# Re-ordering the start of a one-core decoder layer: warm-up operand, the add of the mean squares, five positions in four instruction streams

## The reference

```python
h = rmsnorm(x, norm_pre_g)                       # 512 x 1024
u = h @ w_in                                     # 1024 x 4096: q, k, v, gate of two head groups
a = diff_attention(...) * silu(gate_a)           # 4 heads, two softmax maps each, map0 - lam * map1
b = moba_attention(...) * silu(gate_b)           # 8 heads of 64
y = concat(a, b) @ w_out                         # 1024 x 1024
out = x + rmsnorm(y, norm_post_g)
```

## Time and profile before

| | us |
|---|---|
| median of three runs | 254.41 |
| the profiled execution | 254.41 |
| its span, first to last instruction | 252.5 |
| PE busy in the span | 245.4 (97%) |
| DVE busy | 176.8 (70%) |
| ACT busy | 142.8 (57%) |
| POOL busy | 32.2 (13%) |

### The profile page before, as it was taken

The page is one execution under the profiler, slowest core; times in us unless marked ns, Lnnn a source line. Parts: engine busy times, 40 slices in busy tenths (PEclk is TensorE's granted clock), DMA queues, the critical chain, the costliest instruction groups (busy, mean ns, idle before and its releaser), DMA issues.

```text
span 252.5 us, 4454 instructions
## 1 busy us (share of the span) xinstructions
PE 245.4 (97%) x1569; PEld 123.1 (49%) x1569; DVE 176.8 (70%) x393; ACT 142.8 (57%) x336; POOL 32.2 (13%) x74
## 2 busy tenths in 40 slices
PE   7999999999999999999999999999999999999991
PEld 7444444445454554544455444454444454555570
DVE  2898586487468688868877767977787896835313
ACT  4677566165356667574677595667565665611110
POOL 2129300000000320041032033000000000111101
PEclk9999999999999999999999999999999999999998
DMA  7968989605555544544935654679849769982422
GB/s 241 401 203 189 310 269 378 207 6 135 106 163 159 180 114 128 148 155 115 209 96 134 139 159 120 129 186 170 169 130 220 192 158 167 203 202 43 125 86 83
DMA packets 59674, 42.47 MB, mean 168 GB/s; under 512 B 45808, under 2 KB 46072, under 8 KB 59652
## 3 DMA queue, kind: packets, MB, share of 16 engines
q1 hardware_dynamic: 59636, 42.18, 63.9%
q10 hardware_dynamic: 16, 0.00, 0.0%
HBM read 29.04 MB, written 2.13 MB: 123 GB/s over the span
## 4 chain that ended last, share of the span: by engine, by line
PE 93%; DMA 3%; SPq 1%; DVE 0%; DVEq 0%; issue 0%; POOLq 0%; ACT 0%; POOL 0%; ACTq 0%
PE unit_ps L574 72%; PE score_ps L630 6%; PE o_ps L651 5%; PE unit_ps L604 4%; DMA stage<-in_w_in_dram 3%; PE unit_ps L611 2%; PE unit_ps L585 1%; PE score_ps L703 1%; PE unit_ps L703 1%; SPq L364 0%; PE score_ps L532 0%; SPq L395 0%; DVE area L1052 0%; DVEq L180 0%; POOLq L180 0%
## 5 line engine op out<-in xcount | busy, mean ns | idle before, releaser
L574 PE MATMUL unit_ps<-area,w_hi 128*128 128x512 f16 x256 | 76.2, 379 | 0.0
L782 ACT ACTIVATE arena<-arena,negmax 128x512 f32<-128x512 f32 (+3 forms) x64 | 35.4, 554 | 49.6 <-DVE negmax L979 49.4
L574 PE MATMUL unit_ps<-w_hi,area 128*128 128x512 f16 x192 | 60.3, 379 | 0.0
L574 PE MATMUL unit_ps<-area,w_lo 128*128 128x512 f16 x128 | 48.5, 379 | 0.0
L574 PEld LDWEIGHTS unit_ps<-area,w_hi 128*128 128x128 f16 x256 | 24.1, 98 | 27.2 <-issue 1.1
L574 PE MATMUL unit_ps<-w_lo,area 128*128 128x512 f16 x96 | 36.4, 379 | 0.0
L979 DVE CUSTOM_DVE_ANT_0 arena<-score_ps,strips 128x512 f32<-128x512 f32 (+3 forms) x64 | 28.6, 483 | 9.3 <-PE score_ps L630 9.3
L876 DVE SCALAR_TENSOR_TENSOR w_lo<-stage,g_cols,w_hi 128x512 f16<-128x512 f32 x32 | 24.1, 754 | 10.4 <-ACT w_hi L740 10.3
L574 PEld LDWEIGHTS unit_ps<-w_hi,area 128*128 128x128 f16 x192 | 18.8, 98 | 21.9 <-DVE w_lo L882 0.7
L739 ACT ACTIVATE w_hi<-stage,g_cols 128x512 f16<-128x512 f32 x32 | 22.7, 710 | 6.6 <-DMA stage<-in_w_in_dram 6.4
L878 DVE SCALAR_TENSOR_TENSOR w_lo<-stage,g_cols,w_hi 128x512 f16<-128x512 f32 x32 | 24.8, 776 | 0.0
(11 more groups left out here) (106 smaller groups left out, 356.4 us busy)
## 6 DMA issues: line engine op xcount, KB each, us to landing
stage<-in_w_in_dram SPq DMA_DIRECT2D x32, 512.0 KB, 4.1
stage<-in_w_out_dram SPq DMA_DIRECT2D x8, 512.0 KB, 4.3
arena<-in_x_dram SPq DMA_DIRECT2D x4, 512.0 KB, 8.7
strips<-bias_rows SPq DMA_DIRECT2D x4, 512.0 KB, 4.4
stage<-in_x_dram SPq DMA_DIRECT2D x4, 512.0 KB, 4.4
out_dram<-area SPq DMA_DIRECT2D x3, 512.0 KB, 2.8
strips<-bias_rows SPq DMA_DIRECT2D x1, 1024.0 KB, 7.0
pt<-arena SPq DMA_TRANSPOSE x32, 3.1
```

What stands on the lines that cost most here:

```text
L574: last = nc.tensor.matmul(bank, a, b, start=(k == 0 and n == 0), stop=(k == KT - 1 and n == 2))
L782: nc.scalar.activation(probs[:, i % 2, m, 0:n], probs[:, i % 2, m, 0:n], ACT.Exp, bias=negmax[:, i, m:m + 1], scale=-1.0, accum_out=sums[: ...
```

## The change

It does six things. (1) The warm-up multiplies the identity matrix instead of the tile of ones, seven times instead of eight, and so waits for POOL instead of DVE; DVE's memset is gone. (2) The add of the two halves of the mean square moves from DVE to POOL, ahead of POOL's power, for all four tiles. (3) On ACT unit(0) moves ahead of xn_hi(2), and square(3) behind it. (4) On SP quarter 6 is issued behind both transposes of tile 3, not between them. (5) The four strips go in slots 2, 3, 5, 12 instead of 3, 4, 10, 13. (6) `norm_post_g` is loaded in slot 7 instead of 6.

```diff
--- before.py
+++ after.py
@@ -95,10 +95,10 @@
     quarters = iter((u, q) for u in range(FIRST_UNITS, UNITS) for q in range(4))
     FILL = [tuple([next(quarters) for _ in range(n)] for n in share) for share in shares]
     FILL_END = [[u for part in FILL[j] for u, q in part if q == 3] for j in range(SLOTS)]
-    WARM_UP = 8
+    WARM_UP = 7
     STORE_SLOT = {32: 0, 33: 1}
-    STRIPS_SLOT = {3: 0, 4: 1, 10: 2, 13: 3}
-    GPOST_SLOT = 6
+    STRIPS_SLOT = {2: 0, 3: 1, 5: 2, 12: 3}
+    GPOST_SLOT = 7
     LAST_UNIT = UNITS - 1
     FILL_LAST = [uq for uq in quarters if uq[0] < LAST_UNIT]
     FILL_LAST.sort(key=lambda uq: (uq[0] == LAST_UNIT - 1) * (1 + uq[1] // 2))
@@ -253,7 +253,6 @@
         score_ps = ctx.enter_context(nc.psum_tensor("score_ps", [P, 4, 512], fp32))
         o_ps = ctx.enter_context(nc.psum_tensor("o_ps", [P, 2, 512], fp32))
 
-        warm = gates[:, 1, 2, 0:P]
         x_first = gates[:, 1, 0:2, :].rearrange("p t (k s) -> p (t k) s", s=P)
 
         def x_columns(t):
@@ -283,7 +282,6 @@
         split_lo = sem("split_lo")
 
         consts_ready = sem("consts_ready")
-        warm_ready = sem("warm_ready")
         ident_zero = sem("ident_zero")
         x_squared = sem("x_squared")
         x_half_squared = sem("x_half_squared")
@@ -408,9 +406,9 @@
             load_quarter(5)
             for h in range(2):
                 turn_x(2, h)
-            turn_x(3, 0)
             load_quarter(6)
-            turn_x(3, 1)
+            for h in range(2):
+                turn_x(3, h)
             load_quarter(7)
             load_quarter(8)
             sp.dma_start(lam_in[:, :, :], diff_lambda[0].partition_broadcast(P)).then_inc(lam_loaded, 16)
@@ -466,6 +464,10 @@
             pool.wait_ge(consts_ready, 2)
 
             for t in range(TILES):
+                pool.wait_ge(x_squared, t + 1)
+                pool.wait_ge(x_half_squared, t + 1)
+                nc.gpsimd.tensor_tensor(x_ms[:, t:t + 1], x_sq[:, t:t + 1], x_half_sq[:, t:t + 1], ALU.add)\
+                    .then_inc(x_mean, 1)
                 pool.wait_ge(x_mean, t + 1)
                 nc.gpsimd.tensor_tensor(x_rstd[:, t:t + 1], x_ms[:, t:t + 1], minus_half[:, 0:1],
                                         ALU.pow).then_inc(x_rstd_ready, 1)
@@ -536,7 +538,7 @@
             def warm_up(n):
 
                 for _ in range(n):
-                    nc.tensor.matmul(unit_ps[:, 1, 0:P], warm, warm, start=True, stop=True)
+                    nc.tensor.matmul(unit_ps[:, 1, 0:P], ident[:, :], ident[:, :], start=True, stop=True)
 
             def unit_quarter(u, q):
 
@@ -652,9 +654,8 @@
                                                     start=(k == 0 and n == 0), stop=(k == t and n == 2))
                 last.then_inc(values_done, 1)
 
-            pe.wait_ge(warm_ready, 1)
+            pe.wait_ge(consts_ready, 2)
             warm_up(WARM_UP)
-            pe.wait_ge(consts_ready, 2)
             pe.wait_ge(gpre_loaded, 16)
             nc.tensor.transpose(unit_ps[:, 0, 0:KT], g_rows[:, :], ident[0:KT, 0:KT]).then_inc(g_turned, 1)
             pe.wait_ge(x_loaded[0], 16)
@@ -823,9 +824,9 @@
             split(3)
             x_square(2)
             x_hi(1)
+            unit(0)
+            xn_hi(2)
             x_square(3)
-            xn_hi(2)
-            unit(0)
             xn_hi(3)
             for u in range(1, FIRST_UNITS):
                 for n in SPLIT_AT_UNIT[u]:
@@ -930,13 +931,6 @@
                                                scalar=NORM_EPS, op0=ALU.mult, op1=ALU.add,
                                                accum_out=x_half_sq[:, t:t + 1]).then_inc(x_half_squared, 1)
 
-            def x_mean_square(t):
-
-                dve.wait_ge(x_squared, t + 1)
-                dve.wait_ge(x_half_squared, t + 1)
-                nc.vector.tensor_tensor(x_ms[:, t:t + 1], x_sq[:, t:t + 1], x_half_sq[:, t:t + 1],
-                                        ALU.add).then_inc(x_mean, 1)
-
             def x_norm(t):
 
                 dve.wait_ge(x_rstd_ready, t + 1)
@@ -1054,9 +1048,7 @@
                                                    ALU.add).then_inc(y_ready, 1)
 
 
-            nc.vector.memset(warm, 1.0).then_inc(warm_ready, 1)
             x_half_square(0)
-            x_mean_square(0)
             dve.wait_ge(g_turned, 1)
             nc.vector.tensor_scalar(g_cols[:, :], unit_ps[:, 0, 0:KT], W_SCALE, 1.0, ALU.mult,
                                     ALU.mult).then_inc(g_scaled, 1)
@@ -1066,16 +1058,13 @@
             x_norm(0)
             split(0)
             x_half_square(1)
-            x_mean_square(1)
             split(1)
             x_norm(1)
             split(2)
             x_half_square(2)
-            x_mean_square(2)
             split(3)
             x_lo(1)
             x_half_square(3)
-            x_mean_square(3)
             xn_lo(2)
             unit(0)
             xn_lo(3)
```

## The result

The changed kernel takes 255.58 us (six runs, 255.0 to 256.3) against 254.29 before (six runs, 254.08 to 254.54): a ratio of 1.0055, 95% interval 1.0035 to 1.0077. It is 1.3 us slower, above the predicted 254.83 and above the range's end of 255.4.

The account below looks back on a forecast made before the run. TensorE was taken as the bound, waiting for nothing after 11.02 us, so later delays are paid in full. 254.41 plus 0.42 at unit 2, all else 0, gave 254.83; range 254.3 to 255.4 (8 in 10).

Parts of the forecast that it names:

- the sign: Whole run: slower given 0.39, the same 0.54, faster 0.07; what can't be told from no change is 0.5 us.
- the step that was to bring the 0.42: Tile 2: POOL's held add and power delay xn_hi(2), so unit 2 begins at 21.08 instead of 20.66; bounds 0.06 to 0.8.
- Strips and norm_post_g ... 0: Moved loads on the queue: needed much later, cost 0; bound one load's transfer ahead of one transpose, below 1.4 us.
- The misread step: quarter 6: Load behind tile 3's transposes: issued 23.75, landed 27.25 to 27.95, in time for unit 4 until 28.0, cost 0.
- rival A: Quarter 6 lands behind 28.0 and unit 4 stalls: slower, 255.2 at a landing of 28.4; chance 0.18.
- The add on POOL: Tiles 1 to 3: DVE holds POOL's add to about 0.7 us; x_norm(1) 0.38 late, xn_hi(2) at 16.72, unit 2 0.42 late.
- Rival C: POOL not held for the add, or ACT's new order makes up for it: not slower, 254.4; chance 0.20.
- The warm-up: Start of TensorE: 14 passes from about 1.52 us, transposes of tile 0 0 to 0.1 us later, cost 0.
- the cover: TensorE's wait before 11.02 us for the weights' third quarter: 0.3 us that hides a later start.
- Rival B: Clock rises late, at about 7.8 us, so tile 0's transposes and unit 0's first passes run at half: 255.05; chance 0.10.

Follow-up runs that it names:

- b_load6_behind: Kernel before with quarter 6 issued behind both transposes of tile 3, alone: 254.65 us, ratio 1.0003, beside 254.49.
- b_load6_with_pool_act: Kernel before with the add on POOL, ACT's new order and quarter 6 ahead of both transposes of tile 3: 254.72 us, ratio 1.0009.
- b_warm: Kernel before with the new warm-up alone (seven matmuls on the identity): 254.32 us, ratio 0.9998, beside 254.36.
- b_load6_first: Kernel before with quarter 6 issued ahead of both transposes of tile 3, alone: 254.58 us, ratio 0.9998.
- b_strip_slot12: Kernel before with the fourth strip in slot 12 instead of 13, alone: 254.93 us, ratio 1.0015, beside 254.36.
- b_act_order: Kernel before with ACT's new order alone (unit(0), xn_hi(2), square(3)): 254.52 us, ratio 1.0003, beside 254.50.

## Why the prediction was wrong

It forecast 0.42 us more, gave slower 0.39 against 0.54 for the same, and had the wrong place, the wrong size and one edit misread. That the sign came out right is in part luck: the step that was to bring the 0.42 brought 0.34 alone, not clear of zero, and the largest part of the loss came from a step that was put at nothing. Step by step:

*The step that failed: "Strips and norm_post_g ... 0".* The prediction reasoned that transfers needed much later, in a queue whose work never made TensorE wait, can go anywhere. That looks at the moved transfer and not at what stands behind it. The fourth strip was moved from behind the transpose of step 12 to 1.6 us ahead of it; the transpose came 2.2 us later and had 1.4 of slack. The prediction named the right mechanism as its bound, one load's transfer ahead of one transpose, but put it below 1.4 us where it measured 2.2, wrote "all hidden unless the slack there is smaller", and did not read the slack. The kernel before's trace had it, the landing at 125.0 and the values at 126.39; but slack of 1.4 against a bound below 1.4 would still have said nothing, so it is the price that was too small, and the missing reading only hid how close the two were. This edit alone is 0.57 us (1.0001 to 1.0030), and 0.67 in the changed kernel (255.43 against 254.76). The other three strips did nothing that any run shows: in the trace after they stand 4.2, 3.5 and 2.6 us ahead of the next transpose, and the values of steps 0 to 11 are all 0.79 late, no more than unit 4.

*The misread step: quarter 6.* The description of the change in this document, item 4, and the prediction have it issued behind both transposes of tile 3. The diff has it ahead of both. The price given, for a load that is late, was therefore for another edit; b_load6_behind made that one, and there the figures held roughly: issued 24.3 (forecast 23.75), landed 28.1 (27.25 to 27.95), TensorE at unit 4 waiting 0.2 us, 254.65. That wait is rival A, of a load that is late, at its smallest; the changed kernel has none at unit 4. What the real edit does is the same as with the strip: it puts a load 0.6 us ahead of a transpose that TensorE needs some 5 us later. At the median it is worth 0.39 us in the changed kernel (255.15 against 254.76, not clear of the spread), nothing in the kernel before (254.58 twice), nothing in the company of the POOL and ACT parts (ratios 1.0009 against 1.0008), and nothing with the strip in slot 11 (254.84 against 254.87 with the quarter behind). In single profiles it is 0.5 (the trace after) and 1 us (b_load6_with_pool_act). So this part of the loss is seen in traces and not shown by the times.

*The add on POOL: mechanism right, size too large.* The adds of tiles 1 to 3 took 0.56 to 0.71 us where 0.7 was forecast, and the power of tile 1 ended at 11.84 (forecast 12.1, with the tile 0.16 us earlier). x_norm(1) came 2.47 us behind the tile's arrival on DVE instead of 2.21: 0.26 late, not 0.38. xn_hi(2) began at 16.33 (16.72), unit 2 at 20.91, 0.25 late (0.42). At the end of the run 0.34 us for both parts, within its uncertainty of zero. What the Trainium skill says in "SBUF — State Buffer", section "SBUF: two separate sides", of an exclusive lock held for a whole instruction agrees with the records: each add of tiles 1 to 3 ends about when DVE's two-operand instruction does (10.81 and 10.77 us for tile 1), and the powers of tiles 1 and 2 behind it wait out the next one. Rival C, a POOL that is not held, is out by the same records.

*The warm-up: cost right, cover right.* The transposes of tile 0 came 0.22 us late rather than 0 to 0.1, and the cover took it; b_warm is at 0.9998.

*Rival B, the clock.* It happens, but no run shows that the change brings it. All 14 warm-up records of the changed kernel are at the slow duration, and so are all 16 in most profiles of the old warm-up:

```profile
L541 PE MATMUL unit_ps<-ident x14: 421/421/581, 1.5 to 4.5; 128*128 128x128 f32 x14
```

```profile
L539 PE MATMUL unit_ps<-gates x16: 421/421/580, 1.0 to 4.4; 128*128 128x128 f32 x16
```

The first is the changed kernel, the second b_load6_first, which has the warm-up of before. The profile read for the prediction, with its shortest record of 294 ns, was one of two early ones among ten profiles of the old warm-up (the other is b_strip_slot12's, shortest 274 ns). In the other eight, and in all eight of the new one, the rise came behind the warm-up, in the transposes or in unit 0, and unit 0 began between 6.57 and 6.99 instead of 6.05 and 6.29. Eight of eight against eight of ten is no proof that the new one is later, and b_warm costs nothing. In eleven of these sixteen the spacing of tile 0's transposes falls from 0.21 to 0.11 us within the eight, so the clock did rise in a stretch of transposes, which the prediction had left open. TensorE's clock level in the warm-up is 1.2 GHz by the spacing of 0.21 us between passes of 128 columns, and 2.4 where it is 0.11.

*What is accounted for.* Of the 1.1 to 1.3 us, the strip makes 0.57 to 0.67. Quarter 6 makes between nothing and 0.4. With both as before 0.18 is left, which may be nothing, and with both out of the way in another place 0.38, which is not; how that part divides no run here shows.

## What to carry to other kernels

Where the bound engine never waits, price each moved transfer by the transfers that stand behind it in the same queue: their landing, their reader's start, and the slack between the two, each from the trace of before. Take the price of a load ahead wider than the nearest row gives it (below 1.4 us there, 2.2 here). A slot or two in a list of issues can be worth more than an instruction moved between engines. And read a diff of order twice, once for what leaves a place and once for what is now in front of what.

## What was not expected of the hardware

A transpose issued within 2 us behind a load lands behind that load, however early it is issued: 0.76 to 1.05 us behind it in the eleven pairs that the moved strip and quarter 6 make (125.2 and 125.9 in b_strip_slot12; 26.2 and 27.1 in b_load6_with_pool_act), and up to 2.9 in the other pairs of these profiles (26.5 and 29.4 in b_act_order). The load itself is late too: the fourth strip took 4.2 us in slot 13 of the kernel before, 4.6 to 5.0 in slot 11 and 6.2 to 6.9 in slot 12, with the same quarter ahead of it and a transpose 1.6 us behind. Meanwhile the traffic nearly stops. In the trace after (columns: stretch, its length, clock, DMA share, GB/s):

```profile
123.00:124.00 1.00, 1.00 1.03 377
124.00:125.00 1.00, 1.00 3.08 204
125.00:126.00 1.00, 1.00 0.19 21
126.00:127.00 1.00, 1.00 0.12 19
127.00:128.00 1.00, 1.00 0.70 151
```

For two microseconds 20 GB/s flow while a strip (landing at 127.2) and a transpose (128.0) are both outstanding. The share of 3.08 just before is more than the time there is: a packet counts where it begins, and sixteen that begin there last 2.0 to 2.5 us. The same stretch has one of the 13 packets of the queue called "instruction", at 125.23 us:

```profile
q1 hardware_dynamic: 81, 0.02, 12.9%
q8 instruction: 1, 0.02, 3.0%
```

(queue and kind, packets, MB, share; 125 to 127 us). Such a stop does not need a load ahead: in b_load6_behind, with only transposes of x outstanding, the traffic falls to 18 GB/s from 23 to 24 us, with such a packet at 22.21, and the transpose issued at 19.48 takes 4.8 us. Over the 18 profiles there are 111 stretches of at least 0.6 us with under 40 GB/s while a transfer issued over 2 us before is outstanding; 110 of them begin between 0.2 us ahead of the start of such a packet and 1.4 us behind it. Many of the packets have no such stretch with them, and all 18 profiles have one between the issue and the landing of step 12's transpose, so at step 12 no run here shows how much of the 2.2 us is the strip's bytes and how much the stop. That the packet causes the stop is not shown either, only that they come together: in three of the 110, the one above among them, the traffic falls just before the packet starts.
